# Two orders in the token mixers of a diffusion trunk: GpSimd's exponents against its low parts, VectorE's states against its level factors

## The reference

```python
def step(S, inp):
    qi, ki, vi, gi = inp
    bcum = jnp.cumsum(gi, axis=2)
    b_last = bcum[:, :, -1:, :]
    o_inter = jnp.einsum('bhtd,bhde->bhte', qi * jnp.exp(bcum), S)
    diff = bcum[:, :, :, None, :] - bcum[:, :, None, :, :]
    decay = jnp.where(causal, jnp.exp(jnp.minimum(diff, 0.0)), 0.0)
    att = jnp.einsum('bhtd,bhtsd,bhsd->bhts', qi, decay, ki)
    o = o_inter + jnp.einsum('bhts,bhse->bhte', att, vi)
    S = jnp.exp(b_last[:, :, 0, :])[..., None] * S + jnp.einsum(
        'bhsd,bhse->bhde', ki * jnp.exp(b_last - bcum), vi)
    return S, o
```

## Time and profile before

| what | value |
|---|---|
| median of three runs | 4578.3 us (4576.36 to 4580.62) |
| profiled execution, its own time | 4575.59 us |
| its span | 4573.8 us |
| TensorE busy | 4120.9 us, 90% |
| VectorE busy | 3779.5 us, 83% |
| ScalarE busy | 1645.1 us, 36% |
| GpSimd busy | 1992.2 us, 44% |
| first mixer | from about 203 to 744 us, granted clock 0.92 |
| second mixer | from about 2430 to 2876 us, granted clock 0.87 |

### The profile page before, as it was taken

The page is one execution under the profiler, slowest core; times in us unless marked ns, Lnnn a source line. Parts: engine busy times, 40 slices in busy tenths (PEclk is TensorE's granted clock), DMA queues, the critical chain, the costliest instruction groups (busy, mean ns, idle before and its releaser), DMA issues. The chain is left out here.

```text
span 4573.8 us, 72999 instructions
## 1 busy us (share of the span) xinstructions
PE 4120.9 (90%) x24791; PEld 3718.7 (81%) x24791; DVE 3779.5 (83%) x6714; ACT 1645.1 (36%) x2312; POOL 1992.2 (44%) x1435
## 2 busy tenths in 40 slices
PE   7888987976899999999996887886899999999997
PEld 3588887875799999999996876884779999999996
DVE  7677776599888888999996887488978888899997
ACT  7544443213333333333334443221433333333333
POOL 3233323214555454565653221320745444556663
PEclk9899997988999999999998888987999999999998
DMA  9411111213999999999982110220899999999995
GB/s 371 157 40 55 47 38 70 65 37 81 288 365 361 364 364 356 364 361 364 363 333 68 54 38 22 83 72 11 183 339 361 364 361 362 359 363 363 360 363 209
DMA packets 616028, 1049.50 MB, mean 229 GB/s; under 512 B 229699, under 2 KB 388870, under 8 KB 615430
## 3 DMA queue, kind: packets, MB, share of 16 engines
q1 hardware_dynamic: 467814, 508.86, 32.8%
q0 software_dynamic: 147456, 536.94, 31.6%
q10 hardware_dynamic: 672, 2.62, 0.1%
HBM read 982.75 MB, written 65.54 MB: 229 GB/s over the span
## 5 line engine op out<-in xcount | busy, mean ns | idle before, releaser
L1924 POOL DMA_INDIRECT rows_ex<-in_peer_v,ctx_index x512 | 707.1, 1381 | 476.1 <-DVE row_acc_ex L1999 360.5
L1924 POOL DMA_INDIRECT rows_ex<-in_peer_u,ctx_index x512 | 586.9, 1146 | 628.6 <-DVE dots_ex L2002 500.1
L2085 PE MATMUL pu_ex<-h_hi,uT_hi_ex 128*128 128x384 f32 x2048 | 715.3, 349 | 1.9 <-ACT coef_ex L1949 1.0
L1999 DVE SCALAR_TENSOR_TENSOR row_acc_ex<-rows_ex,factor_ex,row_acc_ex 128x1024 f32<-128x1024 f32 x512 | 657.6, 1284 | 52.8 <-issue 11.2
L2085 PE MATMUL pu_ex<-h_lo,uT_hi_ex 128*128 128x384 f32 x2048 | 692.3, 338 | 0.0
L2085 PE MATMUL pu_ex<-h_hi,uT_lo_ex 128*128 128x384 f32 x2048 | 692.2, 338 | 0.0
L2093 PE MATMUL py_ex<-v_hi_ex,c_hi_ex 128*128 128x512 f32 x1536 | 622.5, 405 | 0.0
L2002 DVE CUSTOM_DVE_ANT_0 rows_ex<-rows_ex,h_row_ex 128x1024 f32<-128x1024 f32 x512 | 604.2, 1216 | 0.0
L2093 PE MATMUL py_ex<-v_lo_ex,c_hi_ex 128*128 128x512 f32 x1536 | 601.0, 391 | 0.0
L2093 PE MATMUL py_ex<-v_hi_ex,c_lo_ex 128*128 128x512 f32 x1536 | 600.6, 391 | 0.0
L1990 DVE TENSOR_TENSOR uT_lo_ex<-pT_ex,uT_hi_ex 128x512 fp32r<-128x512 f32 x512 | 351.5, 686 | 176.0 <-ACT uT_hi_ex L1938 152.3
(11 more groups left out here) (434 smaller groups left out, 8535.6 us busy)
## 6 DMA issues: line engine op xcount, KB each, us to landing
u_raw_ex<-in_peer_u SPq DMA_DIRECT2D x256, 512.0 KB
v_raw_ex<-in_peer_v SPq DMA_DIRECT2D x256, 512.0 KB
ada<-in_ada_w SPq DMA_DIRECT2D x24, 2048.0 KB, 9.8
gates<-stage_ro SPq DMA_DIRECT2D x12, 4096.0 KB, 16.0
g_raw_ex<-gates SPq DMA_DIRECT2D x256, 192.0 KB
w_raw_hgrn<-in_hgrn_w_in SPq DMA_DIRECT2D x40, 512.0 KB
w_raw_re<-in_peer_w_q SPq DMA_DIRECT2D x32, 512.0 KB, 3.7
w_raw_gla<-in_gla_w_in SPq DMA_DIRECT2D x25, 512.0 KB
```

Of the source, the lines that this page charges most:

```text
L1924: pool.indirect_dma_start(out=rows[m % RING][:, :], out_offset=None, in_=a["peer_u" if m < TG * NC else "peer_v"].rearrange("l n d -> (l n ...
L1999: nc.vector.scalar_tensor_tensor(row_acc[g][:, :], rows[j][:, :], factor[:, j:j + 1], row_acc[g][:, :], ALU.mult, ALU.add).then_inc(row_fr ...
L2085: last_ = nc.tensor.matmul(pu[:, 0:TD], w[:, k, :], x[:, k, 0:TD], start=(k == 0 and w is uT_hi[b] and x is h_hi), stop=(k == DC - 1 and w ...
```

## The change

Two edits. On GpSimd the low part of chunk 2 moves from between the exponents of level 0 and level 1 to behind the exponents of all three levels, in both mixers. In the second mixer VectorE makes no level factor ahead of the states (`FIRST` from 3 to 0); the first mixer keeps 4.

```diff
-    FIRST = 3 if mx.gla else 4
+    FIRST = 0 if mx.gla else 4
...
                 for l in range(POOL_LEVELS):
                     exponents(pool.tensor_tensor, l)
                     pool.drain().then_inc(pool_diff, 1)
-                    if l == 0 and (2 < L or not final):
-                        lo(h, 2)
-                for j in range(3, NCH):
+                for j in range(2, NCH):
                     if j < L or not final:
                         lo(h, j)
```

## The result

The changed kernel takes 4540.2 us (median of four runs, 4533.1 to 4542.4) against 4577.6 us (median of four, 4576.4 to 4580.6) for the kernel before: ratio 0.9915, 95% interval 0.9898 to 0.9932. Forecast were 4537 and a range of 4529 to 4572.

What follows compares the result with a forecast made beforehand. VectorE, slowed by GpSimd's low parts, was taken to set the end of the stretch before TensorE's transposes. First mixer -30 and second -11 sum to -41: 4534.6 profiled, 4537 as median; range 4529 to 4572.

Steps and rivals of the forecast that it cites:

- 2 us for each low part that begins before VectorE is through: First mixer, `b_ready` to end of `chunk_factors`: each GpSimd low part begun meanwhile costs VectorE 1.96 us, whatever the order.
- The step that was too sure: First mixer, TensorE at chunk 2: after a 2.8 us wait for its low part, low clock costs 1.7 us.
- rival 1: First mixer: clock stays up, chunk 4's low part may still hit VectorE; if hit, gain 0, total 4567; chance 0.12.
- (a): Second mixer, GpSimd's new order: VectorE gains 1.1 us per steady head (bounds 0 to 2.2); last head 3.2 us shorter.
- (b): Second mixer, `FIRST = 0`, states before level factors: -2.1 and +0.5 us per steady head; bounds -3 to +3.
- Its first term: Second mixer: chunk 1's low part falls beside state updates instead of factor products and costs nothing there, -2.1 us a head.
- The wait that was to be set against it: Second mixer: VectorE stands 2.7 us for the first state product but loses old waits; net +0.5 us a head.
- Half: First mixer: hit avoided, but TensorE's remaining wait leaves low clock through the transposes; 2 us a head, 4553; chance 0.14.
- Nothing: VectorE's total work unchanged, the state chain eats the second mixer's gain; with no first-mixer gain either, 4577; chance 0.07.
- slower: First mixer: low clock after the new wait lasts through chunk 2, transposes and chunk 3; +63 us, 4630; chance 0.05.

Runs made afterwards that it cites:

- the held low part: Changed kernel, second mixer: GpSimd begins chunk 1's low part only when all eight states are made; 4544.5 us, ratio 0.9925.
- The last two experiments: Changed kernel, first mixer: chunk 3's low part held until qk_ready, 4530.8 us; the same with chunk 2's between exponents 1 and 2, 4535.3 us.

## Why the prediction was right, and where it was off

**First mixer: right in mechanism and size.** -30 was forecast, -27.6 measured. VectorE's end at 24.1 (24.2), the wait of 2.8 us (2.6), state products at 32.9 (33.05 in five heads), period 63.3 (63.5 in five heads). "2 us for each low part that begins before VectorE is through" holds for one hit fewer (24.1 with the third held back), for two fewer (22.0) and for more (28.6, where the rule says 28.0, with two more than the changed kernel has). Seven periods of 63.3 would have been 3.1 us less than measured: 1.8 are head 3, which got a low clock at its transposes (65.1), 0.4 head 0, where chunk 2 took 9.5 us behind a wait of 12.0, and the rest 0.16 in each other head.

**The step that was too sure** is that a wait of 2.8 us brings the clock down, from one row at 1.95 us. It did in heads 1, 2 and 5 and not in 3, 4 and 6. Where it did not, rival 1's case was there: chunk 4's low part came at 23.7, and missed the last product, begun at 23.44, by 0.26 us. I had put that margin at 0.2 and given the case 0.12 without asking what the miss alone would give. It gives the same gain. So the forecast held for a reason in half of the heads that was not the one I named, and with a margin that an extra 0.3 us on VectorE would have used up.

**Second mixer: -11 forecast, -15.1 measured,** by terms that were wrong singly. (a) Alone, GpSimd's order was to give 1.1 us in each head and 3.2 in the last. The last head gave 2.8; the other three lost 4.4. The early values were real (1.6 us in head 1), and they moved the whole chain of states, gate products and exponentials; TensorE's low clock in the gate products gave the 1.6 us back, and I had no term for the clock there. I also had chunk 2's low part ready at 14.3; by my own 12.4 for the exponents, 0.25 of drain and 2.82 it is 15.5, and it came at 15.35 in head 2, where TensorE stood 1.47 us for it. (b) Was to give 2.1 - 0.5 = 1.6 us a head. By the medians it gives some 12 us in all where (a) stands beside it (4552.3 against 4540.2). Its first term is exact (2.15, by the held low part). The wait that was to be set against it, 2.7 us for the first state product, came out at 0.6 in heads 1 and 2: TensorE's wait ahead of the value transposes, forecast at 2, was 2.01 in head 1 and the clock stayed up, and in head 2, where TensorE came late from chunk 2, it was 0.3. In head 0 (-0.5 where -2.7 was forecast) TensorE stood 3.1 us for chunk 2's low part, which I saw, with 6.8 us of low clock from then on, and came so late with og1 that VectorE stood 4.39 us for ScalarE, which I had costed at nothing. In two of the experiments the same code had the same wait of 3.1, but 3.4 us of low clock; VectorE stood 0.59 us and the head took 94.6.

**A term put at nothing.** The sum left the rest of the kernel as it was. It grew by 8.0 us between the two traces, at least 2 of them by the clock in the product behind the second mixer. So -42.7 us in the heads, where -41 was forecast, became -34.7 in the span and -37.4 in the medians.

**Rivals.** "Half" is what the third low part held back alone gives (-17.5 us, one wait with its low clock left). "Nothing" and "slower" did not come: the low clock behind the new wait was short: a mean of 0.81 over the 8.9 us of chunk 2, between levels of 0.5 and 1, is some 3.4 us at the lower one. By the Trainium skill, "SBUF — State Buffer", section "Who interferes with whom", VectorE instructions with two SBUF inputs and reading GpSimd instructions exclude each other. The trace agrees (2.96 and 3.01 instead of 0.82). The page adds that a VectorE instruction with at most one SBUF input, outside the two-port modes, does not contend: the states beside the low part agree (0.48 us each, as alone). Reordering gave 27.6 us all the same, since the low part that left the stretch now excludes VectorE where nobody waits for it.

## What to carry to other kernels

Where two engines exclude each other, the work of the second does not vanish by being moved, but it is free wherever the first is off the path: count which of its instructions begin before the first engine's deadline, and hold the others behind the semaphore of that deadline instead of trusting the order to bring them late enough. When a stretch is shortened on one engine, follow the gain through the engines behind it up to the next wait, and price TensorE's work in between at the low clock as well: in this kernel 1.6 us were lost there. And a wait moved in front of covered work is better than the same wait in front of uncovered work, since the low clock behind it is then covered too. The last two experiments show the limit: once chunk 2 had no cover left, the place of the wait made no difference (441.7 and 442.9 us).

## What the runs showed of the hardware that I had not expected

The granted clock behind waits of equal length is not the same. After 2.6 us without work it was down in three of six heads of one trace and up in the other three, with the same work before and behind; after 2.14 us it was down in one head of three. This is not chance from execution to execution: two experiments with the same first mixer (GpSimd's order alone, and chunk 1's low part held back) show it in the same heads, 1, 2 and 5 and then 3. What picks them stays open. After the old wait of 6.8 us it was down every time, and head periods scattered by 1.5 us with how long it stayed so (66.62 to 68.11). With one wait of 4.8 us the seven periods agree within 0.05 us (64.85 to 64.90).
